# GpSimd takes six weight splits, VectorE sums its convolution taps in PSUM and takes ten taps more from TensorE

## The reference

```python
def conformer_conv_module(h, w_pw1, b_pw1, w_dw, b_dw, ln_g, ln_b, w_pw2, b_pw2):
    d = h.shape[-1]
    a = jnp.einsum("bsd,de->bse", h, w_pw1) + b_pw1
    u = a[..., :d] * jax.nn.sigmoid(a[..., d:])
    u = causal_dwconv(u, w_dw, b_dw)
    u = jax.nn.silu(layernorm(u, ln_g, ln_b))
    return jnp.einsum("bsd,de->bse", u, w_pw2) + b_pw2
```

## Time and profile before

| | us |
|---|---|
| median of 3 runs | 1009.12 (1008.51 to 1009.58) |
| the profiled execution, its own time | 1009.79 |
| its span, first to last instruction | 1008.0 |
| TensorE busy in the span | 971.9 (96%) |
| VectorE busy | 595.4 (59%) |
| ScalarE busy | 389.4 (39%) |
| GpSimd busy | 1.1 (0%) |

### The profile page before, as it was taken

One profiled execution on the slowest core, in us unless ns is written; L12 is line 12 of the kernel. 1 busy time (PEld: TensorE's weight loads), 2 busy tenths in 40 slices (PEclk: granted clock), 3 DMA queues, 4 the chain that ended last, 5 costly groups with the idle time before them and its releaser, 6 DMA issues.

```text
span 1008.0 us, 11441 instructions
## 1 busy us (share of the span) xinstructions
PE 971.9 (96%) x4308; PEld 800.2 (79%) x4308; DVE 595.4 (59%) x751; ACT 389.4 (39%) x581; POOL 1.1 (0%) x24
## 2 busy tenths in 40 slices
PE   5999999699999999999999999999999999999994
PEld 4787878488888888888888889788888888888883
DVE  5899999556656655556433338775466555432333
ACT  5748931454433334334222226453343333321220
POOL 0000000000000000000000000000000000000000
PEclk9999999699999999999999999999999999999997
DMA  6220201012232322231232242222323322223212
GB/s 254 93 77 7 84 8 76 1 42 85 85 124 83 122 86 83 87 121 57 86 104 88 95 143 86 84 84 83 125 83 96 112 83 70 86 86 114 86 57 84
DMA packets 15288, 88.50 MB, mean 88 GB/s; under 512 B 1696, under 2 KB 1824, under 8 KB 8224
## 3 DMA queue, kind: packets, MB, share of 16 engines
q1 hardware_dynamic: 15264, 88.19, 25.6%
HBM read 86.09 MB, written 2.10 MB: 87 GB/s over the span
## 4 chain that ended last, share of the span: by engine, by line
PE 95%; DVE 2%; ACT 1%; issue 1%; DMA 0%; DVEq 0%; SPq 0%; ACTq 0%
PE bank L796 28%; PE bank L797 28%; PE bank L798 28%; PE bank L854 2%; PE bank L853 2%; PE bank L855 2%; PE bank L862 1%; PE bank L895 1%; PE bank L868 1%; DVE out_sb L787 0%; DMA x_res<-x 0%; DVE conv_out L650 0%; PE bank L973 0%; PE bank L978 0%; PE bank L977 0%
## 5 line engine op out<-in xcount | busy, mean ns | idle before, releaser
L796 PE MATMUL bank<-h_hi,w_hi 128*128 128x512 f32 x832 | 326.6, 393 | 12.3 <-DVE w_lo L551 11.0
L797 PE MATMUL bank<-h_lo,w_hi 128*128 128x512 f32 x832 | 324.8, 390 | 0.0
L798 PE MATMUL bank<-h_hi,w_lo 128*128 128x512 f32 x832 | 324.8, 390 | 0.0
L520 DVE TENSOR_TENSOR w_lo<-w_raw,w_hi 128x2048 fp32r<-128x2048 f32 (+2 forms) x89 | 180.2, 2027 | 104.1 <-ACT w_hi L310 102.5
L310 ACT ACTIVATE w_hi<-w_raw 128x2048 fp32r<-128x2048 f32 (+2 forms) x88 | 148.8, 1695 | 209.8 <-PE bank L798 209.8
L796 PEld LDWEIGHTS bank<-h_hi,w_hi 128*128 128x128 f32 x832 | 156.9, 189 | 46.4 <-issue 13.0
L797 PEld LDWEIGHTS bank<-h_lo,w_hi 128*128 128x128 f32 x832 | 156.9, 189 | 33.2 <-issue 0.7
L798 PEld LDWEIGHTS bank<-h_hi,w_lo 128*128 128x128 f32 x832 | 156.8, 188 | 32.7
L797 PE MATMUL bank<-u_lo,w_hi 128*128 128x512 f32 x416 | 162.8, 391 | 0.0
L796 PE MATMUL bank<-u_hi,w_hi 128*128 128x512 f32 x352 | 136.9, 389 | 0.0
L798 PE MATMUL bank<-u_hi,w_lo 128*128 128x512 f32 x352 | 136.9, 389 | 0.0
(11 more groups left out here) (122 smaller groups left out, 810.4 us busy)
## 6 DMA issues: line engine op xcount, KB each, us to landing
w_raw<-w_up SPq DMA_DIRECT2D x44, 1024.0 KB, 4.8
w_raw<-w_down SPq DMA_DIRECT2D x32, 704.0 KB, 4.1
w_raw<-w_pw SPq DMA_DIRECT2D x11, 1024.0 KB, 5.6
x_res<-x SPq DMA_DIRECT2D x4, 512.0 KB, 7.7
out<-out_sb SPq DMA_DIRECT2D x8, 256.0 KB, 2.7
w_raw<-w_pw SPq DMA_DIRECT2D x2, 512.0 KB, 6.0
w_raw<-w_pool SPq DMA_DIRECT2D x2, 512.0 KB, 3.7
band_raw<-band SPq DMA_DIRECT2D x1, 800.0 KB, 5.8
```

The costliest lines, as they stand in the source:

```text
L520: V.tensor_tensor(w_lo[s][:, 0:columns], w_raw[s][:, 0:columns], as_f32(w_hi[s][:, 0:columns]), SUB).then_inc(w_split[s], 1)
L796: M.matmul(dst, a, hi, start=start, stop=False)
L797: M.matmul(dst, a, lo, start=False, stop=False)
L798: return M.matmul(dst, b, hi, start=False, stop=stop)
```

## The change

- GpSimd runs the six splits of the units 2, 3 and 4 of both slots (steps 2 and 3 of the first map, and the first units of the second map), each after waiting for ScalarE's rounding. VectorE's splits of these units are gone.
- VectorE's taps sum in PSUM: bank 4 for the first tile of a step and bank 7 for the second. The last tap (30) writes `conv_out` in SBUF from the bank.
- TensorE takes 11, 11, 11 and 13 taps per tile instead of 12, 12, 12 and 15; VectorE takes the rest, five per tile and ten in all more. ScalarE's diagonals fall to match.
- The bank of the mean is 2 instead of 7. It is one of the map's banks, so all mean sums come after the last drain of it: those of steps 0 and 1 stand together behind the taps of step 2.

```diff
-PE_TAPS = [12, 12, 12, 15]
-
-DIAG_TAPS = [12, 12]
+PE_TAPS = [11, 11, 11, 13]
+
+DIAG_TAPS = [11, 11]
 EXTRA_TAPS = PE_TAPS[3] - DIAG_TAPS[1]
 
-SPLIT_TAPS = 26
 EARLY_TAPS = 22
 
-BANK_SUM, BANK_MEAN = 4, 7
+BANK_SUM, BANK_MEAN = 4, 2
+
+BANKS_ACC = (4, 7)
+
+POOL_SPLITS = range(M_PW1 + 2, M_PW2 + 1)
...
+            for m in POOL_SPLITS:
+                for s in range(2):
+                    pool.wait_ge(w_rounded[s], m + 1)
+                    nc.gpsimd.tensor_tensor(w_lo[s][:, :], w_raw[s][:, :], as_f32(w_hi[s][:, :]), SUB).then_inc(w_split[s], 1)
...
+                        acc = bank[BANKS_ACC[t]][:, :]
                         if k == PE_TAPS[i]:
-                            V.tensor_scalar(conv_out[:, c, :], src, w, col("b_dw", c), MUL, ADD).then_inc(tap_step[t], 1)
+                            V.tensor_scalar(acc, src, w, col("b_dw", c), MUL, ADD).then_inc(tap_step[t], 1)
                         else:
                             dve.wait_ge(tap_step[t], steps_before[i] + k - PE_TAPS[i])
-                            V.scalar_tensor_tensor(conv_out[:, c, :], src, w, conv_out[:, c, :], MUL, ADD).then_inc(tap_step[t], 1)
+                            V.scalar_tensor_tensor(acc if k < TAPS - 1 else conv_out[:, c, :], src, w, acc, MUL, ADD).then_inc(tap_step[t], 1)
...
-                    taps(0, first=EARLY_TAPS, last=SPLIT_TAPS)
-                    for s in range(2):
-                        split_unit(s, M_PW1 + 2, UNIT)
-                    taps(0, first=SPLIT_TAPS)
+                    taps(0, first=EARLY_TAPS)
...
-                for s in ((1,), (), (0, 1), (0, 1))[i]:
-                    split_unit(s, M_PW1 + i + 1, UNIT)
+                if i == 0:
+                    split_unit(1, M_PW1 + 1, UNIT)
...
-                if i >= 2:
-                    sum_for_mean(i - 2)
                 if i:
                     tensor_taps(i - 1)
+            wait_drained((BANK_MEAN,), DRAINED_PW1 + PW1_STEPS)
+            sum_for_mean(0)
+            sum_for_mean(1)
             tensor_taps(PW1_STEPS - 1)
```

## The result

| | before | changed |
|---|---|---|
| median of the runs | 1009.01 us (4 runs, 1008.51 to 1009.58) | 1016.27 us (4 runs, 1015.04 to 1016.61) |
| the profiled execution, its own time | 1009.79 us | 1016.32 us |
| its span | 1008.0 us | 1014.5 us |

The ratio is 1.0069, with an interval of 1.0057 to 1.0082: slower by 0.7%, where 1004.7 us was forecast. The range ended at 1015.5 us.

A forecast was written before the change was run, and what follows sets the result against it. TensorE and VectorE were taken as full together in the convolution stage; walking VectorE's drains and the last mean products, the mean came at 176.74 instead of 181.15 us, -4.4 us, so 1009.12 became 1004.7 us, range 1001.5 to 1015.5.

The forecast's parts named there:

- the turn of steps 2 and 3: VectorE, drain to low part of glu: bound by ScalarE's chain; -2.74 us in step 2, -1.17 in step 3.
- the two engines block each other: Rival: GpSimd's splits hold VectorE's low parts of glu, 2.0 and 4.0 us in steps 2 and 3: 1010.7 us; chance 0.20.
- long form: Block rival's longer case: in step 2 another split slips between the low part's halves, 4.4 us more: 1015.1 us; chance 0.08.
- The last sums: End of the stage: two mean products of 0.86 us and 0.16 latency behind VectorE, ending at 176.74 against 181.15 us.
- The removed splits and added taps of step 1: VectorE, step 1: splits gone -4.40, two more taps +1.33, dearer first taps +0.41; next drain moves by -2.66 us.
- The PSUM accumulator: VectorE's taps: reading and writing a PSUM bank costs 0, with bounds of plus and minus 0.067 us.
- The first tap with a bank: VectorE, first tap of a step (541 ns before): priced as a tap, 0.2 us more each, 0.41 per step.
- GpSimd's split: Each weight split on GpSimd: 4.4 us, twice VectorE's; nothing lost up to some 7 us.
- PSUM as accumulator is dearer: Rival: VectorE's taps cost 0.067 us more each, 10.2 us in all: 1014.9 us; chance 0.14.
- GpSimd is late: Rival: at 13.4 us a split TensorE waits for GpSimd, last product near 186 instead of 181: 1014 us; chance 0.08.
- VectorE is quicker on PSUM: Rival: VectorE's stage is shorter than thought and TensorE's chain bounds, -6.4 us: 1002.7 us; chance 0.08.
- Nothing moves: Rival: partial forms of the other rivals use up the 4.4 us: 1008 to 1010 us; chance 0.08.

The follow-up runs named there:

- e1: Changed kernel, but in steps 2 and 3 GpSimd starts its splits only after both low parts of glu are written: 1008.69 us, ratio 0.9999.
- e5: Changed kernel with each GpSimd split issued as four instructions of 128x512 instead of one of 128x2048: 1007.07 us, ratio 0.9986.
- e6: Changed kernel with the taps summed in SBUF (conv_out) as before, instead of PSUM: 1024.53 us, ratio 1.0159.
- e3: Changed kernel with all six splits back on VectorE, the rest of the change kept: 1011.45 us, ratio 1.0031.
- e7: Changed kernel plus 18 unused TensorE products into bank 3 before the last mean sums: 1015.89 us, ratio 1.0068.
- e4: Kernel before with only the taps summed in PSUM and the mean sums moved; splits and tap shares as before: 1009.23 us, ratio 1.0002.
- e2: Changed kernel, but in steps 2 and 3 VectorE splits slot 0 and GpSimd splits slot 1 after the low parts of glu: 1004.59 us, ratio 0.9960.
- e8: e2 with ScalarE making the eight extra diagonals of step 3 after glu's high part instead of before it: 1002.30 us, ratio 0.9934.
- the square: Table of ratios, splits on VectorE against shared: taps as before 1.0002 (e4), 1.0001; ten taps more on VectorE 1.0031 (e3), 0.9960 (e2), 0.9934 (e8).

## Why the prediction was wrong, and where it was right

**The step that failed** is the turn of steps 2 and 3, from the drain to the low part of glu. The forecast let `glu_lo` start when ScalarE was done and take its 1.36 us for two. It did start then (2.45 and 4.78 us of idle, forecast 2.7 and 5), and was held for 6.6 and 4.2 us. This was written down as the rival "the two engines block each other", whose long form gave 1015.1 us and had a chance of 0.08. It had 2.0 + 4.4 us for step 2 and 4.0 for step 3, so its prices hold. The error is one of weight. I set against it that "only four instructions on the path are exposed". But by my own times these instructions came right inside GpSimd's splits. The Trainium skill (SBUF — State Buffer, Who interferes with whom) says that the second of the two to come is fully blocked. The runs agree in three ways: apart from the splits a pair takes 1.36 us again (e1), beside quarters the hold shrinks to 1.1 us (e5), and a tap with two SBUF inputs is held to 5.1 us (e6). "No row here can say" was no reason for as little as one in five.

**What no case had:** the tail. The last sums were priced at 1.88 us in every case. But TensorE's holes were 5.86 and 4.34 us long, and behind the second its clock was at half: +1.9 us in the stage. That takes only a VectorE that is late, not a block: e3 has a hole of 4.18 us and the same 3.78 us of sums. Behind the first hole some nine products ran slowly too, at no cost, since VectorE was the later one by far.

The kernel went past the range by 0.8 us. The tail alone isn't shown to be the reason: with its sums quick, in e7, the kernel took 1015.89 us, still outside. Beside the long form's 1015.1 us, the stage lost 2.1 us more (12.5 instead of 10.4, the 1.9 us among them), 1.55 us came back outside it (0.94 + 0.61), and 0.6 us is the median's distance from the profiled execution (0.05 us here, taken as 0.67).

**What held.** The removed splits and added taps of step 1: -2.66 forecast, -2.80 measured. The PSUM accumulator: priced at nothing with bounds of 0.067 us on either side, measured 749 ns against 745 and 0.66 us from start to start. The Trainium skill (VectorE: DVE Perf Modes, The TRN2 errata) has 120 + N cycles with PSUM against 58 + N, by which, as an estimate, it would have been 65 ns more. Neither these rows nor e4 show that. The first tap with a bank, priced like a tap, is even a little dearer:

```profile
L600 DVE TENSOR_SCALAR bank<-glu,par 128x512 f32<-128x512 f32 x8 | 6.1, 804 | 0.0
```

That is 804 ns against 541 in SBUF. GpSimd's split: 4.4 us taken, 4.5 to 4.6 measured. The Trainium skill (GPSIMD Engine Reference, Performance versus the Vector engine) has 4497 ns for an addition of 2048 float32 columns, and the rows agree with it. TensorE's wait for the second pair: 0.6 forecast, 0.83 measured. The sum of all of it, with the block taken away, is e2: -4.55 us against -4.4 in the stage. That its median, 1004.59, also lies 0.1 us from 1004.7 is in part luck: its interval alone is 2.7 us wide. The rivals "PSUM as accumulator is dearer" and "GpSimd is late" fell, the first by e4, the second by the 0.83 us; of "VectorE is quicker on PSUM" hardly anything shows (from start to start a queue of taps went from 0.663 to 0.658 us each, some 0.6 us in all), and "Nothing moves" is excluded by the interval.

**A part whose worth no sum had:** the accumulators in PSUM came out free, as forecast. That they leave the taps one SBUF input stood only among the reasons against the block, without a number. e6 shows that without them the change would have cost 8.3 us more.

## What to carry to other kernels

Before work is put on a GpSimd that "does nothing", list which VectorE instructions run beside it and how many SBUF tensors each reads; a handful of short ones on the path can cost more than the moved work saves (here three were held, for 10.8 us in all). The ways out that worked here: let the two not meet (e2, e8), keep one operand in PSUM (e6 against the changed kernel), or cut the long instruction into pieces (e5). And where two engines are full together, relieve the one and move load from the other onto it in the same change: either alone gained nothing here, as the square shows.

## What the hardware showed that I had not expected

- The block looks like work. The held instruction counts as busy (5144 ns for a `glu_lo` of 0.7 us) and the views name no releaser for it. What gives it away is a duration far from that of its like, as here for the changed kernel (shortest, median, longest in ns):

```profile
L644 DVE TENSOR_TENSOR glu_lo<-glu,glu_hi x8: 710/724/5144, 42.1 to 158.1; 128x542 fp32r<-128x542 f32 x8
```

- Both sides are held. In step 2 GpSimd's second split lasted 5.12 us instead of some 4.57, and then VectorE's next one waited for all of it. In e6 the pair beside the SBUF taps lasted 10.03 us instead of 9.21. Whether turn-taking of this kind is a rule, these few cases don't tell.
- The granted clock moves a cost as much as it makes one: after 4.34 us (changed kernel, before 184.47) and 4.46 us (e1, before 115.52) without work TensorE ran at 0.50 and 0.52 of full speed; after 2.33 us (e2, before 173.38) its sums took 1.98 us, nearly undisturbed. Yet of the 1.8 us that quick sums saved in e7, 1 us was paid back 20 us later.
